# Forgetting attention: where in its step the tensor engine turns the rounds of values and keys

## What is computed

```
y = rmsnorm(h) @ w_in          # q_a | k_a | v_a | f | q_b | k_b | v_b | gate_a | gate_b
lf = log_sigmoid(f + b);  c = cumsum(lf)
s = q_a . k_a / 8 + c_q - c_k, masked to key <= query      # 8 heads of 64
o_a = softmax(s) @ v_a
outputs, among others: fox_k_p, fox_v_p = k_a, v_a of the 1040 keys, a row for each token
```

## Time and profile before

| | |
|---|---|
| median of 3 runs | 1664.07 us |
| profiled execution | 1662.88 us, its span 1661.1 us |
| branch A of the prompt | 76 to 360 us of the span |
| PE busy in the whole span | 1638.8 us, 99% |
| DVE, ACT, POOL busy | 65%, 47%, 21% |
| granted TensorE clock, mean | 0.999 |

### The profile page before, as it was taken

How to read it: one execution, slowest core, us unless ns; L and a number is a source line. 1 busy time by engine, 2 the same in 40 slices (tenths; PEclk the granted TensorE clock), 3 DMA queues, 4 the chain that set the end, 5 groups by cost and what they waited for, 6 DMA issues and landing times.

```text
span 1661.1 us, 27363 instructions
## 1 busy us (share of the span) xinstructions
PE 1638.8 (99%) x9476; PEld 1484.0 (89%) x9476; DVE 1082.1 (65%) x2320; ACT 774.6 (47%) x1630; POOL 346.6 (21%) x503
## 2 busy tenths in 40 slices
PE   8999999999999999999999999999999999999998
PEld 8999999999999989989988998888888888888886
DVE  7566666635999544364445597778887668774744
ACT  6487887865778433342234333222222434343521
POOL 1323333234322322234533120000000000000242
PEclk9999999999999999999999999999999999999999
DMA  5222212322222554563334332344443764444541
GB/s 181 80 62 58 62 48 60 98 81 69 68 68 58 189 164 162 171 218 124 133 127 127 115 108 97 119 145 134 143 145 131 247 208 116 127 152 123 190 165 76
DMA packets 164347, 205.43 MB, mean 124 GB/s; under 512 B 16168, under 2 KB 113256, under 8 KB 164240
## 3 DMA queue, kind: packets, MB, share of 16 engines
q1 hardware_dynamic: 164240, 204.04, 38.3%
HBM read 144.88 MB, written 57.32 MB: 122 GB/s over the span
## 4 chain that ended last, share of the span: by engine, by line
PE 81%; DVE 9%; issue 4%; ACT 3%; POOL 2%; DMA 1%; SPq 0%; DVEq 0%; POOLq 0%; ACTq 0%
PE gb L543 8%; PE gb L2400 5%; PE sc L3283 5%; PE gb L3283 5%; PE gb L2935 4%; PE gb L2771 4%; PE sc L2935 4%; PE tp L2935 4%; PE tp L3283 4%; PE gb L993 3%; PE gb L994 3%; PE gb L995 3%; PE tp L842 3%; PE sc L2559 3%; PE tp L2559 3%
## 5 line engine op out<-in xcount | busy, mean ns | idle before, releaser
L513 POOL TENSOR_TENSOR wl<-raw,wh 128x256 fp32r<-128x256 f32 x168 | 125.1, 776 | 260.7 <-ACT wh L498 173.5
L993 PE MATMUL gb<-Xh,wh 128*128 128x384 f32 (+1 forms) x504 | 173.1, 343 | 0.0
L994 PE MATMUL gb<-Xh,wl 128*128 128x384 f32 (+1 forms) x504 | 170.9, 339 | 0.0
L995 PE MATMUL gb<-Xl,wh 128*128 128x384 f32 (+1 forms) x504 | 170.9, 339 | 0.0
L3407 POOL TENSOR_TENSOR wl<-raw,wh 128x1024 fp32r<-128x1024 f32 x2 | 5.3, 2628 | 559.6 <-ACT wh L3398 559.6
L543 PE MATMUL gb<-Xh,wh 128*128 128x384 f32 (+1 forms) x288 | 104.0, 361 | 0.0
L543 PE MATMUL gb<-Xh,wl 128*128 128x384 f32 (+1 forms) x288 | 97.6, 339 | 0.0
L543 PE MATMUL gb<-Xl,wh 128*128 128x384 f32 (+1 forms) x288 | 97.4, 338 | 0.0
L993 PEld LDWEIGHTS gb<-Xh,wh 128*128 128x128 f32 x504 | 94.9, 188 | 0.4
L994 PEld LDWEIGHTS gb<-Xh,wl 128*128 128x128 f32 x504 | 94.9, 188 | 0.1
L995 PEld LDWEIGHTS gb<-Xl,wh 128*128 128x128 f32 x504 | 94.8, 188 | 0.0
(11 more groups left out here) (569 smaller groups left out, 4764.5 us busy)
## 6 DMA issues: line engine op xcount, KB each, us to landing
zr<-u_scr SPq DMA_DIRECT2D x91, 256.0 KB, 3.0
raw<-in_w_in SPq DMA_DIRECT2D x70, 256.0 KB, 3.3
u_scr<-ustore SPq DMA_DIRECT2D x26, 576.0 KB, 4.5
u_scr<-ustore SPq DMA_DIRECT2D x13, 768.0 KB, 3.2
sig_scr<-sig SPq DMA_DIRECT2D x16, 576.0 KB, 3.1
raw<-in_w_up SPq DMA_DIRECT2D x36, 256.0 KB, 4.5
kc<-in_cache_fox_k SPq DMA_DIRECT2D x8, 1024.0 KB, 5.7
vc<-in_cache_fox_v SPq DMA_DIRECT2D x8, 1024.0 KB, 7.6
```

What stands on the lines that cost most here:

```text
L513: last = nc.gpsimd.tensor_tensor(wl[U.slot][:, q], raw[U.slot][:, q], wh[U.slot][:, q].bitcast(F32), ALU.subtract)
L993: nc.tensor.matmul(bank[:, 0:x1 - x0], wh[U.slot][:, ws], Xh3[:, k, x0:x1], start=(k == 0), stop=False)
L994: nc.tensor.matmul(bank[:, 0:x1 - x0], wl[U.slot][:, ws], Xh3[:, k, x0:x1], start=False, stop=False)
L995: last = nc.tensor.matmul(bank[:, 0:x1 - x0], wh[U.slot][:, ws], Xl3[:, k, x0:x1], start=False, stop=(k == KT - 1))
```

## The change

The three V rounds and the three K rounds of each pair are issued directly behind the first P rounds of their step, ahead of the values product, the scores and all fills. Before, a V round stood behind two fills behind the scores, and a K round at the very end of its step. The numbers of the rounds, their banks, their readers on ACT and DVE and the order of these readers are as before; so are all other engines' programs.

```diff
                 for j in range(min(turns, 2)):
                     fox_turn_pe(pe, n, j)
+                if p < 4 and t in (2, 3, 4):
+                    v_round_pe(pe, p, t - 2)
+                if p < 4 and t in (5, 6, 7):
+                    k_round_pe(pe, p, t - 5)
                 if s >= 4 and s % 2 == 0:
                     fox_values_pe(pe, s // 2 - 2)
...
                     fox_turn_pe(pe, n, 2)
-                if p < 4 and t in (2, 3, 4):
-                    m = min(at_ + 2, fill)
-                    fill_pe(pe, FOX_FILL, FOX_FILL_UNITS, s, at_, m)
-                    at_ = m
-                    v_round_pe(pe, p, t - 2)
                 fill_pe(pe, FOX_FILL, FOX_FILL_UNITS, s, at_, fill)
-                if p < 4 and t in (5, 6, 7):
-                    k_round_pe(pe, p, t - 5)
```

## The result

The changed kernel takes 1671.23 us (median of 5 runs, 1669.84 to 1672.67) against 1663.99 for the kernel before on the same chip: +7.2 us, ratio 1.0044 with a 95% interval of 1.0033 to 1.0054. The profiled execution took 1669.84, its span is 1668.0.

A forecast was written before the change was run, and what follows sets the result against it. The prediction took PE, busy 99% of the span, as the bound; bank waits of 1.98 us in pair 0 and 3 x 2.07 in pairs 1 to 3 gave 8.2 on 1664.07, so 1672.3, range 1666.8 to 1676.5.

The forecast's parts named there:

- the slip of the chain: ACT and DVE from V0's reading to V2's reading: each starts 0.38 us later, bounds 0 and 0.44.
- PE's own work: nothing: PE in branch A: no instruction added or removed, 24 rounds move; taken as nothing, 1.0 us kept for the range.
- K0 (item 21): Pair 1, step 21: K0 waits for V2's bank until 161.98, leaving PE 1.13 us late.
- K1 (item 22): Pair 1, step 22: K1 waits 0.85 us for K0's bank, leaving PE 1.98 us late.
- K2 (item 23): Pair 1, step 23: K2 waits 0.11 us for K1's bank; PE is then 1.99 us late.
- P at t = 8 (item 24): Pair 1, step 24: P comes 1.99 us late, its second round 0.08 more, so the pair loses 2.07.
- the other two signs of being wrong: K0 starting within 0.1 us of P's end, or branch A ending less than 3 us later.
- V2: Pairs 1 to 3: V2 waits some 0.2 us for the t = 3 P round's bank, inside K0's 1.13.
- Only K0 waits: Rival for branch A: K0 alone waits, K1 and K2 find banks free; 1666.8 us, chance 0.12.
- The faster rival: Rival at t = 5: V rounds read earlier, so waits of 0.9 and exits of 1.0 vanish; 1662.2 us, chance 0.03.
- nothing waits: Rival: a reader or shared bank was misplaced in the account, so no wait appears; 1664 us, chance 0.06.
- The clock: Rival: waits amid transposes lower PE's clock at t = 5 of every pair, 1.9 us each; 1680 us, chance 0.02.

The follow-up runs named there:

- V rounds only: The changed kernel with the K rounds back at the end of their step, only V rounds behind P; 1664.61 us against 1664.27 for the kernel before.
- only K read ahead of exp: The changed kernel, but ACT reads K rounds ahead of the step's exp and V rounds still behind it; 1666.92 us against 1664.32 for the kernel before.
- keys split a step later: The changed kernel with ACT's and DVE's splitting of the next head's keys at t = 6 and 14; 1679.04 us against 1663.75 for the kernel before.
- POOL swapped: The kernel before, but POOL prepares item s+2's edge mask ahead of zeroing item s's tail; 1664.96 us against 1664.15 unedited.
- keys split behind K0's reading: The changed kernel, but ACT's key splitting at t = 5 and 13 stands behind its V and K reading; 1671.31 us, kernel before 1664.15.
- kernel before read ahead of exp: The kernel before, PE's order kept, but ACT reads each step's V or K round ahead of the exp; 1672.64 us against 1664.15 unedited.

## Why the prediction was right, point by point

The forecast was 1672.3 against a median of 1664.07, +8.2; measured are +7.2. The mechanism, three K rounds that wait for banks read late, came out as told; one term of the sum, the slip of the chain, was mis-sized.

**PE's own work: nothing.** Right: the same matmuls, and busy time 1640.4 against 1638.8. The 1.6 more are no work: a transpose is listed with 0.27 us or more although the next one starts 0.11 behind it, so the first part of each wait counts as busy (K0 of pair 1: 0.62 listed as idle, the scores 0.83 late). The 0.08 for an exit that I kept for the range is not there either: the kernel with V rounds only is 0.06 ahead at item 63, less than its lead of 0.20 at item 0.

**The terms of pair 1**, as the lateness of the scores behind each round, with moved blocks and the lateness at item 16 taken off:

| | worked out | measured |
|---|---|---|
| K0 (item 21) | 1.13 | 0.83 |
| K1 (item 22) | 1.98 | 1.75 |
| K2 (item 23) | 1.99 | 1.82 |
| P at t = 8 (item 24) | 2.07 | 1.82 |

The step that was mis-sized is the slip of the chain of ACT and DVE. By the prediction's own words ("if the chain makes up the slip") this step was wrong, though the other two signs of being wrong did not show. It was 0.38 in the prediction, 0.26 at V0's reading because I took the exp's end with its accumulator read as the time at which ACT goes on, and 0.02 at V2's reader because DVE's splitting of the queries lost its overlap with POOL. "From there to V2's reading each of ACT and DVE starts on the end of the other" was true of the order and false of the lengths: I carried a duration over in which a third engine had a part. The wait at K0 stayed because most of it needs no slip: 0.75 of the 1.13 was the lower bound. K0 started 0.12 behind the end of V2's reader where I had allowed 0.05. The head of the chain was read rightly, although the row of the minimum names POOL and not the scores: POOL and the scores ended together there (149.70 and 149.69), and in the kernel after the row names the scores, again 0.76 behind them (151.12 and 151.88). K1 added 0.92 where I had 0.85 and K2 0.07 where I had nearly nothing. The last 0.08, for P's readers, did not come.

**V2.** I expected a wait of 0.2 in pairs 1 to 3. There was none: in pair 1 P's four blocks began at 157.48, V2 at 157.92, four times 0.11 behind, and in pairs 2 and 3 it is 0.44 too. The missing slip explains it: the reader of that bank (line 1293) ended at 157.78 against 156.18 before, 1.60 later, where item 16 was 1.57 later.

**The rivals.** Only K0 waits: no, though the kernel that reads K ahead of exp comes to just this case, with +2.6 us where I had worked out 2.7 for it. The faster rival failed in this kernel by the reason given: the reader's place did not move. Where it was moved too, the faster case came about, at -1.0 us against the -1.9 worked out. That nothing waits: ruled out by the rows above. The clock: granted 1.00 in the stretch with the waits, 0.999 in the whole. That alone does not settle it, because the granted clock is also listed as 1.00 in the slow start of the kernel before (the third value from the end of the line below, 3 to 6 us). The pace does: behind the wait at K0 four transposes took 0.38 us to the next matmul, behind the wait at K1 0.41 (168.65 to 169.06). At the pace of the start, 0.21 apiece (one starts at 4.60 us, the third after it at 5.24), it would be 0.85.

```profile
3.00:6.00 3.00, 3.00 (x15) 3.00 (x16) 0.00 (x0) 1.23 (x3) 0.00 (x0) 1.00 0.92 287
```

```profile
163.29 0.63 PE L842 MATMUL tp<-ident,nB 128*128 128x128 f32 x4 [0.62 <-DVE Vs L1362]
163.67 0.43 PE L1186 MATMUL sc<-kk,qs 128*128 128x400 f32 x1
```

The rule of the Trainium skill (TensorE: Matmul & The Clock Gate, Part 4: PE-mode transpose), that the high clock does not engage for transposes, has no trace here; waits of up to 0.9 us amid transposes cost no more than themselves.

**What K1's wait is.** The prediction gave K1's wait as the time to K0's reading, with the split of the keys in it. That is the instruction waited for, but not a term that can be taken out: with the split moved behind the reading, the same delay came one step later. The cause that the runs bear out is the work that stands on ACT between the late exp at t = 5 and K1's reading, 8.4 us in a row: with the same work but K read ahead of it (only K read ahead of exp), and with the split taken out of it (keys split a step later), the added waits of K1 and K2 go. How much of it is ACT's part of the split and how much the reciprocal that stands behind DVE's part was not parted. In the changed kernel the exp at t = 6 starts at 172.60, when both ACT's own work (172.56) and the minimum (172.57) have just ended, so the scores that come late behind K1 hold it as much as ACT does.

## What to carry to other kernels

Here a producer that was moved earlier gained nothing while its reader kept its place; it only asked for its bank sooner. Before moving such a round, write down for each bank when the reader before it ends, and move reader and round together. And when a wait follows one instruction, test whether the engine's whole row is too long before crediting that instruction: here the same delay reappeared a step later.

## What the runs showed of the hardware

In this kernel a DVE subtraction with both operands in SBUF and a POOL tensor operation on SBUF hold each other up, whichever starts first. The split of line 1134 took 0.67 to 0.69 us alone; started 0.26 us behind a POOL operation it ended 0.55 us behind that one's end (152.76 + 0.60 = 153.36 and 153.02 + 0.89 = 153.91 before; 152.72 + 0.68 = 153.40 and 152.98 + 0.97 = 153.95 with POOL swapped). The other order stands in the kernel before:

```profile
129.58 1.23 DVE L1154 TENSOR_TENSOR kk<-nB,kk 64x1040 fp32r<-64x1040 f32 x1 [1.28 <-ACT kk L1147]
129.67 0.19 POOL L1264 MEMSET u<- 128x112 f32 x1 [2.28 <-PE gb L842]
129.82 1.36 POOL L1220 TENSOR_TENSOR bias<-bias 128x144 f32<-128x144 f32 x1
```

DVE, which was first, kept its 1.23 us; POOL's operation, 0.50 us elsewhere at this width, took 1.36 and ended 0.37 behind DVE. POOL's memset kept its 0.19 us. DVE's line 1327, of whose two operands one lies in PSUM, took 0.41 to 0.42 us with or without such a POOL operation beside it.

The Trainium skill (SBUF — State Buffer, section "SBUF: two separate sides") says that DVE, in an operation with two SBUF inputs, and a GpSimd operation that reads SBUF hold a shared port pair exclusively, so that the later one waits for the end of the earlier. The trace agrees in both orders, and so do the memset, which reads nothing, and line 1327. Only the length of the wait is a little under a full one: from the end of POOL's operation the split needed 0.55 us, not 0.67.

The second point is the signal: in the changed kernel the weight load behind an ACT or DVE reader started 0.05 to 0.06 us behind the reader's listed end at K1, K2 and the second P round of t = 5, but 0.11 to 0.12 behind it at K0. It is not K0 alone: where the first P round of a step waits for line 1293, it is 0.12 as well (173.22 with the keys split behind K0's reading, 175.25 with the kernel before read ahead of exp). What makes the two values was not tried.
